# Sample state products between the matmuls of a block, low parts ahead of other vector work, and a norm factor by Ln and Exp, in a hybrid decoder step

## What is computed

```python
u = xn @ w_in                                   # 1024 -> x, B, C, conv value and gate, z, dt, gates
a = glu_v * jax.nn.sigmoid(glu_g)
a = causal_dwconv(a_full, conf_dw_w, conf_dw_b) # 31 taps a channel ("Conformer taps")
...
xbc = jax.nn.silu(causal_dwconv(xbc_full, ssm_conv_w, ssm_conv_b))   # 4 taps
...
def ssd_chunk(h, x, dt, A, bm, cm):
    ...
    y = jnp.einsum('btsgh,bsghp->btghp', w, x)
    y = y + jnp.einsum('btgn,bghpn->btghp', cm, h) * jnp.exp(cum)[..., None]
    tail = jnp.exp(cum[:, -1:] - cum) * dt
    h_new = jnp.exp(cum[:, -1])[..., None, None] * h + jnp.einsum('bsgh,bsgn,bsghp->bghpn', tail, bm, x)
    return h_new, y
...
y = y.reshape(bsz, length, D_INNER) * jax.nn.silu(z.astype(f32))
yg = y.reshape(bsz, length, SSM_NORM_GROUPS, D_INNER // SSM_NORM_GROUPS)
yg = yg * lax.rsqrt(jnp.mean(yg * yg, axis=-1, keepdims=True) + EPS)
```

## Time and profile before

| | |
|---|---|
| median of 3 runs | 1598.5 us (1597.8 to 1607.1) |
| the profiled execution, its own time | 1598.62 us |
| its span, from first to last instruction | 1596.9 us |
| TensorE's mean granted clock | 0.92 of full |
| TensorE, VectorE, ScalarE, GpSimd busy | 86%, 74%, 51%, 13% |
| waits of TensorE for low parts | 29.1 us in 14 times |

### The profile page before, as it was taken

The page is one execution under the profiler, slowest core; times in us unless marked ns, Lnnn a source line. Parts: engine busy times, 40 slices in busy tenths (PEclk is TensorE's granted clock), DMA queues, the critical chain, the costliest instruction groups (busy, mean ns, idle before and its releaser), DMA issues. The chain is left out here.

```text
span 1596.9 us, 25982 instructions
## 1 busy us (share of the span) xinstructions
PE 1378.5 (86%) x8618; PEld 1219.4 (76%) x8618; DVE 1175.7 (74%) x1634; ACT 813.0 (51%) x1427; POOL 212.3 (13%) x328
## 2 busy tenths in 40 slices
PE   4989899998999989999892899997359999999980
PEld 4988888888888888888881799985348777777760
DVE  4557987888878788887876454542748999999964
ACT  4353554534545345462541332322138999999961
POOL 1011030210202102021120000000201111111112
PEclk9988998999999899998995999999669999999995
DMA  6141624426144261442713824311678999999936
GB/s 190 52 115 55 188 63 121 114 78 177 47 121 113 72 184 47 136 108 80 192 42 123 249 66 161 116 53 34 267 278 305 361 368 367 370 365 367 369 113 237
DMA packets 191724, 273.98 MB, mean 172 GB/s; under 512 B 15661, under 2 KB 154117, under 8 KB 175252
## 3 DMA queue, kind: packets, MB, share of 16 engines
q1 hardware_dynamic: 179100, 248.36, 46.7%
q0 software_dynamic: 9536, 17.98, 3.2%
q10 hardware_dynamic: 3040, 7.03, 1.2%
HBM read 238.21 MB, written 52.48 MB: 182 GB/s over the span
## 5 line engine op out<-in xcount | busy, mean ns | idle before, releaser
L868 PE MATMUL pu<-xh,wh 128*128 128x304 f32 (+1 forms) x1280 | 294.9, 313 | 31.3 <-DVE wl L237 29.1
L868 PE MATMUL pu<-xl,wh 128*128 128x304 f32 (+1 forms) x1280 | 282.2, 303 | 0.0
L868 PE MATMUL pu<-xh,wl 128*128 128x304 f32 (+1 forms) x1280 | 281.5, 303 | 0.0
L868 PEld LDWEIGHTS pu<-xh,wh 128*128 128x128 f32 x1280 | 210.2, 202 | 47.6 <-DVE wl L237 36.0
L868 PEld LDWEIGHTS pu<-xl,wh 128*128 128x128 f32 x1280 | 210.2, 201 | 0.0
L868 PEld LDWEIGHTS pu<-xh,wl 128*128 128x128 f32 x1280 | 209.0, 200 | 0.0
L1003 DVE SCALAR_TENSOR_TENSOR cacc<-a_p,gc,cacc 128x528 f32<-128x528 f32 x232 | 188.4, 812 | 5.8
L526 ACT ACTIVATE wh<-ring 128x1024 fp32r<-128x1024 f32 x80 | 84.5, 1057 | 211.1 <-PE pu L868 207.2
L1713 DVE TENSOR_TENSOR W13l<-W,W13h 128x1024 fp32r<-128x1024 f32 x160 | 185.0, 1217 | 7.0 <-issue 6.5
L1697 ACT ACTIVATE W13h<-W 128x1024 fp32r<-128x1024 f32 x160 | 156.3, 1064 | 0.2 <-issue 0.2
L2132 PE MATMUL eh<-W13h,xch 128*128 128x512 f32 x320 | 130.5, 408 | 14.7 <-DVE xcl L2219 10.2
(11 more groups left out here) (394 smaller groups left out, 2644.0 us busy)
## 6 DMA issues: line engine op xcount, KB each, us to landing
W<-in_exp_w SPq DMA_DIRECT2D x100, 1024.0 KB, 7.2
ring<-in_w_in SPq DMA_DIRECT2D x80, 512.0 KB, 4.1
x<-in_exp_w SPq DMA_DIRECT2D x20, 1024.0 KB, 7.7
stage<-decay_rows SPq DMA_DIRECT2D x8, 1120.0 KB, 6.6
x<-in_state_ssm SPq DMA_DIRECT2D x16, 512.0 KB, 6.3
out_new_ssm_sample<-x SPq DMA_DIRECT2D x16, 512.0 KB, 5.3
wraw<-in_ssm_out_w SPq DMA_DIRECT2D x8, 1024.0 KB, 7.4
Ed<-decay_rows SPq DMA_DIRECT2D x32, 140.0 KB, 6.9
```

Of the source, the lines that this page charges most:

```text
L868: last = pe.matmul(u_cols(r, a, b), w[:, k % RING, j, :], x[:, j, a:b], start=(j == 0 and n == 0), stop=(j == KD - 1 and n == 2))
```

## The change

- The **sample products** leave `stage2(5)` and become four parts `samples(r)` of four products each, with one `j` step of block 9 (6 matmuls) between them. Block 9's first half is also cut, between `states_turned(2)` and `(3)`.
- The **state additions** leave the end of the group and stand in the next group's block 0, one after every two `j` steps; VectorE's new states (`states_new`) move with them to the start of the next group. After the last group both stand alone.
- The **norm factor** is no longer a square root on ScalarE and a reciprocal on VectorE, but Ln and Exp on ScalarE: two of each group's ScalarE instructions stay, with another function, and one of 560 columns is added. The number of table loads in a group stays at two: the second one, for Exp, now stands in `closing`, where before it stood at the next tanh.
- **Low parts** of blocks 3 to 6 are made earlier in VectorE's order, ahead of `scaled`, `silu` and trailing taps.
- **21 taps** instead of 17 are done in the group itself, and 10 trail. The last two trailing instructions now stand behind the low part of block 6 and the samples' silu.
- `conf_samples` works in `cv` instead of `ybuf`, no longer waits for the norm, and stands at the start of the next group (in the last group: before its end).

```diff
 DVE_STEPS = 59
-TRAIL = 14
+TRAIL = 10
...
         s_cvs, s_ths, s_sum, s_root = map(sem, ("s_cvs", "s_ths", "s_sum", "s_root"))
-        s_ds0, s_dsr, s_settled = sem("s_ds0"), sem("s_dsr"), sem("s_settled")
+        s_csum, s_ds0, s_dsr, s_settled = sem("s_csum"), sem("s_ds0"), sem("s_dsr"), sem("s_settled")
...
                     act.wait_ge(s_sum, 2 * g + r + 1)
-                    act.activation(zc[:, 0, 280 * r:280 * r + 280], turn[r][:, 0:280], ACT.Sqrt,
+                    act.activation(zc[:, 0, 280 * r:280 * r + 280], turn[r][:, 0:280], ACT.Ln,
                                    scale=1.0 / (2 * P), bias=eps[:, :]).then_inc(s_root, 1)
+                act.wait_ge(s_root, 2 * g + 2)
+                act.activation(zc[:, 1, :], zc[:, 0, :], ACT.Exp, scale=-0.5).then_inc(s_rec, 1)
...
                     evac(q)
+                    if q == 2 and not is_first:
+                        act.wait_ge(s_csum, g)
...
+            def states_added(g, r):
...
+                pe.wait_ge(s_Bblk, g + 1)
+                if r < 2:
+                    pe.wait_ge(s_h0tev, 4 * g + r + 3)
+                else:
+                    pe.wait_ge(s_hnew, 4 * g + r)
+                i, q = r // 2, r % 2
+                pe.matmul(turn[r % 2][:, :], xtl[0:SAMP, 1, 2 * i:2 * i + 2, :],
+                          Bblk[:, 4 * q:4 * q + 4, :], start=True, stop=True).then_inc(s_hs, 1)
...
-                def block(k, halves=(0, 1)):
+                def block(k, first=0, end=KD):
...
                     r = U_OF[k]
-                    for h in halves:
-                        if h == 0:
-                            free(r)
-                            low_done(pe, g, k)
-                        for j in range(4 * h, 4 * h + 4):
-                            for n, (w, x) in enumerate(((wh, xh), (wh, xl), (wl, xh))):
-                                for a, b in ((0, USPLIT), (USPLIT, T)):
-                                    last = pe.matmul(u_cols(r, a, b), w[:, k % RING, j, :], x[:, j, a:b],
-                                                     start=(j == 0 and n == 0), stop=(j == KD - 1 and n == 2))
-                        if h == 1:
-                            last.then_inc(s_u, 1)
+                    if first == 0:
+                        free(r)
+                        low_done(pe, g, k)
+                    for j in range(first, end):
+                        for n, (w, x) in enumerate(((wh, xh), (wh, xl), (wl, xh))):
+                            for a, b in ((0, USPLIT), (USPLIT, T)):
+                                last = pe.matmul(u_cols(r, a, b), w[:, k % RING, j, :], x[:, j, a:b],
+                                                 start=(j == 0 and n == 0), stop=(j == KD - 1 and n == 2))
+                    if end == KD:
+                        last.then_inc(s_u, 1)
...
                                       start=True, stop=True)
-                    if ci == 0:
-                        pe.wait_ge(s_h0tev, 4 * g + 4)
-                        for i in range(2):
-                            for b in range(NSAMP):
-                                last = pe.matmul(pC[:, P * i + TSAMP * b:P * i + TSAMP * b + TSAMP],
-                                                 h0T[:, i, b, :], cv[:, 3, TSAMP * b:TSAMP * b + TSAMP],
-                                                 start=True, stop=True)
-                    else:
-                        last = pe.matmul(pC[:, 2 * P:4 * P], Tt[0:S, j % 2, 0, :], xtl[0:S, j % 2, :, :], start=True, stop=True)
-                    last.then_inc(s_pe2, 1)
+                    if ci:
+                        pe.matmul(pC[:, 2 * P:4 * P], Tt[0:S, j % 2, 0, :], xtl[0:S, j % 2, :, :], start=True,
+                                  stop=True).then_inc(s_pe2, 1)
...
+                def samples(r):
...
+                    i, q = r // 2, r % 2
+                    pe.wait_ge(s_h0tev, 4 * g + r + 1)
+                    if r == 0:
+                        pe.wait_ge(s_y, 6 * g + 6)
+                    for b in range(4 * q, 4 * q + 4):
+                        c = P * i + TSAMP * b
+                        last = pe.matmul(pC[:, c:c + TSAMP], h0T[:, i, b, :], cv[:, 3, TSAMP * b:TSAMP * b + TSAMP],
+                                         start=True, stop=True)
+                    if r == 3:
+                        last.then_inc(s_pe2, 1)
...
-                def states_added(r):
...
-                block(0)
                 if is_first:
+                    block(0)
...
                 else:
+                    for k in range(4):
+                        block(0, 2 * k, 2 * k + 2)
+                        states_added(g - 1, k)
...
-                block(6, (0,))
+                block(6, 0, 4)
...
                 stage1(1)
-                block(6, (1,))
+                block(6, 4)
...
                 stage1(2)
-                block(7, (0,))
+                block(7, 0, 4)
...
                 stage1(3)
-                block(7, (1,))
+                block(7, 4)
...
                 stage1(4)
-                block(8, (0,))
+                block(8, 0, 4)
...
                 states_turned(0)
-                block(8, (1,))
+                block(8, 4)
...
                 states_turned(1)
-                block(9, (0,))
+                block(9, 0, 2)
                 states_turned(2)
+                block(9, 2, 4)
                 states_turned(3)
+                samples(0)
+                block(9, 4, 5)
+                samples(1)
+                block(9, 5, 6)
                 stage2(5)
-                block(9, (1,))
-                for r in range(4):
-                    states_added(r)
+                samples(2)
+                block(9, 6, 7)
+                samples(3)
+                block(9, 7)
...
                 group(g1 + 1)
+            for r in range(4):
+                states_added(G - 1, r)
...
+            def states_new(g, rs):
...
+                for r in rs:
+                    dve.wait_ge(s_hs, 4 * g + r + 2)
+                    dve.wait_ge(s_h0t, 4 * g + 4)
+                    for b in range(4):
+                        bb, i = 4 * (r % 2) + b, r // 2
+                        last = stt(h0[:, i, bb, :], h0[:, i, bb, :],
+                                   Ed[:, i, TSAMP * bb + TSAMP - 1:TSAMP * bb + TSAMP],
+                                   turn[r % 2][:, P * b:P * b + P])
+                    last.then_inc(s_hnew, 1)
...
-                    dve.wait_ge(s_yn, 2 * g + 2 + 1)
...
                     seen = bass.AP(src.tensor, src.offset, [src.ap[0], [n, NSAMP], [1, TSAMP], [1, CK]])
-                    prod = ybuf[:, :, :].rearrange("p i t -> p (i t)")[:, 0:SAMP * CK]
+                    prod = cv[:, 2:4, :].rearrange("p q t -> p (q t)")[:, 0:SAMP * CK]
...
                     k.link(dve.tensor_reduce(csum[:, :], prod.rearrange("p (s j) -> p s j", j=CK), AX_X, ALU.add))
+                    dve.sem_inc(s_csum, 1)
...
-                for r in range(2):
-                    dve.wait_ge(s_root, 2 * g + r + 1)
-                dve.reciprocal(zc[:, 1, :], zc[:, 0, :]).then_inc(s_rec, 1)
...
                 behind, ahead = iter(range(CK - TRAIL, CK)), iter(range(CK - TRAIL))
-                trail(4)
+                if not is_first:
+                    states_new(g - 1, (0,))
+                    conf_samples(g - 1)
+                    states_new(g - 1, (1,))
+                trail(2)
+                if not is_first:
+                    states_new(g - 1, (2, 3))
+                trail(1)
...
                 split(g, 2)
+                trail(3)
...
                 ssm_conv(0)
-                trail(2)
+                split(g, 3)
...
                 silu(0)
-                split(g, 3)
...
                     decays()
-                if not is_first:
-                    conf_samples(g - 1)
-                trail(2)
+                split(g, 4)
                 silu(1)
-                split(g, 4)
+                trail(1)
                 ssm_conv(2)
-                trail(3)
+                split(g, 5)
                 silu(2)
-                split(g, 5)
+                trail(1)
...
                 ssm_samples()
-                trail(3)
-                assert is_first or next(behind, None) is None
+                split(g, 6)
...
                 silu_s()
-                split(g, 6)
+                trail(2)
+                assert is_first or next(behind, None) is None
...
                 for j in range(5):
-                    taps(2)
+                    taps(3 if j in (1, 2) else 2)
...
                 k.link(stt(zc[:, :, :], th[:, :, :], 1.0, zc[:, :, :], ALU.add, ALU.mult))
-                taps(4)
+                taps(3)
...
-                for r in range(4):
-                    dve.wait_ge(s_hs, 4 * g + r + 2)
...
-                    last.then_inc(s_hnew, 1)
+                taps(3)
...
+                if is_last:
+                    conf_samples(g)
...
             group(G - 1, is_last=True)
```

(5 more changed lines are left out.)

14 lines of the change are left out of this document (removed).

## The result

The changed kernel takes 1588.4 us (median, 1585.7 to 1591.2), the kernel before in the same runs 1599.7 us. The ratio is 0.9922, with an interval of 0.9903 to 0.9941: 0.8% faster, where I had forecast 1566 us and a range that ended at 1590. The profiled execution took 1590.2 us with a span of 1588.5.

The account below looks back on a forecast made before the run. VectorE's order bounds blocks 1 to 5, TensorE and its clock the stretch to the sums. -29 - 4.5 + 22 - 11 - 11.5 + 2.4 = -32 us, from 1598.6 to 1566 us (1556 to 1582); range 1543 to 1590 us.

Parts of the forecast that it names:

- State additions in block 0: From sample products to sums: TensorE needs 12.1 us, VectorE's queue 14.2 us, so the sums wait 2 us for VectorE.
- Low parts earlier: Blocks 1 to 6: both waits a group for low parts go, -29 us, and half clock behind them, -4.5 us.
- the last trailing tap: Around block 6: late `aout` delays `decay(0)` some 4 us, making TensorE wait; +3.1 us a group, +22 us.
- The clock term: Behind the low-part waits: half clock, seen in three of seven groups, goes with them; 3 x 1.5 = -4.5 us.
- State additions and the clock: Last turned states to end of sums: 22.7 us at full clock plus 1.9 for clock, against 26.2; -11 us over 7.
- Sample products between steps: Group's end: four parts, three steps and small products take 6.6 us instead of 5.6, leaving one step of block 9 behind.
- End of the trunk: Last sample products to last `aout`: 22.8 us instead of 35.3, with sample products ending 1.0 us later; -11.5 us.
- Norm factor: Between sums and scale: ScalarE's two instructions and table load end before VectorE wants the result inside the groups.
- Group 0: First group: block 3's low part ahead of `steps()` makes TensorE's turning of rows 1.6 us late; with third tap +2.4 us.
- the fourth: Rival: waits before `stage2(0)` and `stage2(2)` bring half clock, or block 6's low part is late; 1587 us, chance 0.12.

Follow-up runs that it names:

- e2: The kernel before, with block 0 waiting only until ScalarE has read the buffer it takes (block 8), not block 9 too; 1601.3 us, ratio 1.0002.
- e14: The changed kernel with its wide wait of block 0, but the four state additions in a row at a group's end as before; 1551.9 us, ratio 0.9721.
- e1: The changed kernel, but block 0 waits only until block 8 has been read, no longer for block 9; 1542.5 us, ratio 0.9631.
- e4: The kernel before with only low parts 3 to 6 and the taps in new places, ten trailing taps instead of fourteen; 1599.8 us, ratio 0.9993.
- e12: The changed kernel with block 0's narrow wait, but low parts 3 to 6 and the fourteen trailing taps in the old order; 1542.8 us, ratio 0.9613.
- e13: The kernel before with only the norm factor by Ln and Exp and the pair on `csum` at the head of a group's queue; 1567.4 us, ratio 0.9810.
- e9: The changed kernel with block 0's narrow wait and the last two trailing taps, `aout` among them, ahead of block 6's low part; 1544.7 us, ratio 0.9632.
- e7: The changed kernel with block 0's narrow wait, but the sixteen sample products in one row behind the last chunk, as before; 1539.6 us, ratio 0.9598.
- e6: The changed kernel with block 0's narrow wait, but the norm factor again by Sqrt on ScalarE and reciprocal on VectorE; 1557.8 us, ratio 0.9712.
- e3: The changed kernel, but in group 0 alone VectorE's queue has the order of the kernel before; 1584.3 us, ratio 0.9887.
- e11: The changed kernel with its wide wait of block 0, but ScalarE reads block 9 ahead of the squares; 1566.4 us, ratio 0.9748.

## Why the prediction was wrong

**The step that failed** is "State additions in block 0". It counted TensorE's way from the sample products to the sums as "0.8 + 6.3 + 4 x 1.0 + 1.0" and set against it only VectorE's queue. Between the 0.8 (the rest of block 9) and the 6.3 (block 0) stands block 0's start condition, and I didn't ask who meets it. In the kernel before four state additions stood there, 4.5 to 6 us, and ScalarE read block 9 meanwhile; e2 shows that the wide wait cost nothing then, e14 that it costs nothing with the additions in place, e1 that it costs 46 us without them. The cover was moved, and I costed its removal at nothing. The runs show in its place 28.6 us of waits in 7 times, which with the half clock behind them make the short stretches 48.3 us longer.

**Low parts earlier (-29, and -4.5 of clock)** and **the last trailing tap (+22)** were one thing cut in two. Together I had -11.5, the measured long stretches give -28.5. The waits for `wl` went as said; but e4 shows that the order gives 0 us by itself, e12 that it is worth some 5 to 6 us once the work is out, and e13 that the work taken out gives 17.5 of the 28.5. What gives the rest isn't shown. The prediction named that work and put the whole -29 on the waits that would go. The +22 rested on a delay of 4 us of `decay(0)` and 3.1 us a group. The timeline of the changed kernel has `aout` 1.7 us after the start of block 6, as walked, but GpSimd's four copies behind it take 0.8 us instead of the 2.1 that I read from the earlier trace rows. Most of that is one copy, before and after:

```profile
490.53 1.19 POOL L445 COPY gcum<-cums 128x24 f32 x1
```

```profile
497.91 0.22 POOL L438 COPY gc<-cs 128x37 f32 x1 [50.08 <-DVE aout L1023]
...
498.40 0.20 POOL L445 COPY gcum<-cums 128x24 f32 x1
498.54 0.20 POOL L446 COPY gdt<-dtt 128x24 f32 x1
...
498.78 0.90 ACT L678 ACTIVATE Lx<-stage,gcum 16x16 f32<-16x16 f32 x4 [1.23 <-POOL gdt L446]
```

Before, VectorE was making a low part beside that copy; now it stands idle beside it. Whether this is the reason wasn't tried. `decay(0)` starts 2.9 us after block 6, not 4. What came to TensorE was 1.0 us a group, and less waiting for `hT` in return (5.9 for 8.2 us); e9 shows that an early `aout` gains nothing. The clock term had the wrong sign: a piece at 0.98 stands now in six of seven long stretches, and in three before.

**State additions and the clock (-11)**: +27.4 measured, -20.9 with the wait narrowed. The walk of VectorE's queue was right (the sums waited for `x` by up to 1.6 us where I said 2), and the clock cost less than the 1.9 us that I took: e1's 23.2 us a group stand 0.5 above the 22.7 at full clock. **Sample products between steps** I had as a means to keep the clock up; e7 finds no gain in it. Nor does a row of sixteen drop the clock "each time" within itself: in the kernel before it does so in five groups of seven, and in the other two right behind the row.

**End of the trunk (-11.5)**: -10.3. From the last sample product to the last `aout` 24.3 us, where I had 22.8:

```profile
854.94 0.49 ACT L592 ACTIVATE zc<-pS,eps 128x280 f32<-128x280 f32 x1 [1.35 <-PE pS L862]
855.45 1.28 ACT L595 ACT_TABLE_LOAD   x1
```

```profile
849.58 1.12 DVE L1023 SCALAR_TENSOR_TENSOR x<-x,Ed,pS 128x128 f32<-128x128 f32 x4 [0.58 <-PE pS L844]
850.62 5.59 DVE L1023 SCALAR_TENSOR_TENSOR cacc<-a_p,gc,cacc 128x528 f32<-128x528 f32 x7
857.50 1.51 DVE L1023 SCALAR_TENSOR_TENSOR yout<-ybuf,gc,zc 128x560 f32<-128x560 f32 x2 [1.30 <-ACT zc L595]
```

The sums behind the last new state take 4.2 us (850.7 to 854.94), at a clock of 0.52, where I had 3.0 for them. The 1.3 us of idle time ahead of `yout` are as long as the table load between Ln and Exp, which was in my sum already. The Trainium skill ("ScalarE: Activation LUTs", section "Table sets: the hidden batching unit") has Ln and Exp in one set, so that one load would do; the trace has two, one ahead of Ln and one ahead of Exp, each of 1.28 us, in all eight groups. **Norm factor**: hidden inside the groups, as said, and by e6 worth 15 us; I had counted it only as a part of the low parts and of the end of the trunk. **Group 0 (+2.4)**: +6.9. The low part of block 3 waited until 57.5 us and VectorE's steps behind it started 4.5 us later than before, not 1.6; but 1.3 of these us stood already ahead of the first moved instruction, and e3 gets 3.7 of the 6.9 back.

Of the rivals the fourth ("new waits eat it", 1587 us) has the right time by other waits than it named, and that the range reached to 1590 was luck. Without the overlooked wait the kernel takes 1542.5 us (e1), and my 1566 were 23 us too high for that: half of the 46 us was hidden by pessimism elsewhere.

## What to carry to other kernels

When a piece of work is moved from between two others, look at what the later one waits for, with every instruction in the queue of the engine that meets it; the piece may have been hiding a wait that the profile doesn't show, and a semaphore that counts all buffers where one is needed can then cost what it had not before. Where two engines run neck and neck, as TensorE and VectorE do here, a new order may give little more than another name to the same wait (0 us by itself, 5 to 6 with the work taken out): compare the busy time of the engine waited for, and take work out of it (17.5 us in the same stretches). And price a new wait of TensorE twice: here 23 us of idle time brought 25 us of half clock with it.

## What the hardware showed unexpectedly

After waits of the same length (1.8 us, e11) the clock took several courses: it stayed up (23.65 us for the stretch), it was low for one piece (25.0 us, in three of seven), or it stayed at 1.2 GHz for all of block 0 with TensorE busy 21.45 of 21.45 us (36.25 us); two more stretches lie between (28.3 and 32.4 us). e11's times lie between 1558.2 and 1573.4 us, the changed kernel's, whose wait is 4.3 us, between 1585.7 and 1591.2; that the clock's courses make the wider spread is likely but wasn't shown. What decides between the courses was not settled.
